# One 8 MB transfer per expert for the gate-up weights, in place of four of 2 MB

## The chip, the cores and the metric

The kernel runs on one core of one Trainium2 chip. The metric is the device time in microseconds (us) of one execution, as the median of several runs. The core has five engines that matter here: PE (TensorE, the matrix products), DVE (VectorE), ACT (ScalarE), POOL (GpSimd) and SP (SyncE), which computes nothing and issues the transfers from device memory (HBM) to on-chip memory (SBUF, 128 partitions). A transfer is spread over 16 DMA engines. They work through what SP has issued in the order of issue; each transfer adds to a semaphore when it has landed.

## The reference, cut to what matters

One decoder layer on 256 tokens of width 1024 in float32: a Mamba-2 mixer, a memory cross-attention, and a mixture of 32 experts of which each token takes four. Only the last part is touched, and it takes three quarters of the time, since all experts' weights have to be read once (8 MB of gate-up and 4 MB of down for each):

```
hn = rms_norm(h, ffn_norm)                       # 256 x 1024
top4 of hn @ w_router + b_router, gates = softmax(top logits)
for each expert e, for its tokens:
    gu   = hn @ w_gate_up[e] + b_gate_up[e]      # 1024 -> 2048
    act  = (clip(up) + 1) * gate * sigmoid(1.702 * gate)
    y   += gates[e] * (act @ w_down[e] + b_down[e])   # 1024 -> 1024
out = rms_norm(h + y, final_norm)
```

## The kernel before, in words

**Tiling.** An expert's tokens (up to 64 here) are gathered by a product of the normed tokens `xn` with a one-hot matrix, into `xs`: eight blocks of 128 features by 64 tokens. `gate_up` multiplies these eight blocks with eight blocks of 128 rows of the expert's 1024 x 2048 matrix; that is 64 products with 512 columns. `down` does the same with the activations and 32 products, `scatter` adds the gated result to the sums of all tokens.

**Which row lies on which partition.** The gate-up matrix of an expert is loaded as four pieces `s` = 0 to 3 of 256 rows, 2 MB each. Partition p gets the neighbouring rows 2p and 2p+1 of a piece, 16 KB that lie together in HBM. The normed tokens are written in an order that fits this (`norm_apply`, L1453: features dealt by two neighbours), and the gathers pick their blocks of `xn` by an index `k`.

**Buffers.** Even experts' pieces go to four slots of 16 KB per partition in `ring`; odd experts' pieces to four slots in three places: `mid` (two), the last third of `wring`, and `hs`. The down matrix has one set of two slots of 2 MB. So two experts' gate-up and one expert's down fit.

**Order on SP.** SP issues transfers in program order and waits before each until its slot has been read. `gu_used` counts pieces of gate-up that PE has used, `dn_used` pieces of down. From expert 3 on, a loop issues gate-up of expert e+2 (four transfers, each as soon as PE has used that piece of expert e; L362) and down of expert e (two transfers, each when that half of expert e-1's down has been used; L365). After the loop comes an order written out by hand: pieces 0 and 1 of gate-up 27, down 25, pieces 2 and 3 of gate-up 27, and then down 26, gate-up 28, down 27, gate-up 29, down 28, gate-up 30, down 29, gate-up 31. The down matrices of experts 30 and 31 come last, as eight transfers of 1 MB into the slots of gate-up 30 (L478).

**Order on PE.** For each expert c (`regular`): gate-up of c (L952; it waits for each piece at its first use), in odd experts half a gather (L928), down of c-1 (L980), the transposes of c's result (L967), scatter of c-1 (L990), in odd experts the other half of a gather. At the end `last_experts`: gate-up 31, then the four quarters of down 30 with the transposes between (L1003, L967, L1020), down 31 with the two scatters.

The functions that the change touches, with the numbers of the lines:

Of the kernel before, what the change touches and what calls it, by code (L numbers as in the profile page):

```python
# [55 lines left out]
GP, DP = 4, 2  # L56
RSLOTS = 8
# [5 lines left out]
def build(nc, x, mem, mixer_norm, xattn_norm, mem_norm, ffn_norm, w_in, conv_w, conv_b, dt_bias, a_log,  # L63
          d_skip, ssd_norm, w_out, xa_w_q, xa_w_kv, xa_w_o, w_router, b_router, w_gate_up, b_gate_up,
          w_down, b_down, final_norm, out):
    with ExitStack() as ctx:
# [16 lines left out]
        sq_at = hs_at + 4 * 2048  # L83

# [12 lines left out]

        act_lo = nc.alloc_sbuf_tensor_at("act_lo", [P, 12288], F32R, offset=ring_at)
# [258 lines left out]
        gu_dram = w_gate_up.rearrange("e (s p k) n -> e s p k n", p=P, k=2)  # L357
        dn_dram = w_down.rearrange("e (s p k) n -> e s p k n", p=P, k=4)

        def load_gate_up(sp, e, odd, s):  # L360
            n = GP * odd + s
            sp.dma_start(gu_w(n), gu_dram[e, s, :, :, :]).then_inc(g_ready[n], 16)  # L362
# [4 lines left out]
        def load_gate_up_row(sp, e, odd, s, kk):  # L367
            n = GP * odd + s
            sp.dma_start(gu_w(n)[:, kk:kk + 1, :], gu_dram[e, s, :, kk:kk + 1, :]).then_inc(g_ready[n], 16)
# [4 lines left out]

        def g_loads(n, c):


            return c // 2 + 1 + (1 if n > GP else 0 if n == GP or c < 2 else 1 if n else 2)
# [9 lines left out]
        def _(sp):  # L388
# [33 lines left out]
            load_gate_up(sp, 1, 1, 0)  # L422
# [5 lines left out]
            load_gate_up_row(sp, 1, 1, 1, 0)  # L428
            load_gate_up_row(sp, 1, 1, 2, 0)
            sp.wait_ge(wo_ps, 10)  # L430
            load_gate_up_row(sp, 1, 1, 1, 1)
# [6 lines left out]
            for a in range(2):  # L438
                sp.wait_ge(gu_part, a + 1)
                sp.dma_start(gu_w(0)[:, 0:1, 1024 * a:1024 * (a + 1)],  # L440
                             gu_dram[2, 0, :, 0:1, 1024 * a:1024 * (a + 1)]).then_inc(g_ready[0], 16)
# [20 lines left out]
            with sp.Fori(0, PAIRS - 4, 1) as i:  # L462
# [6 lines left out]
            for e in range(NE - 6, NE - 2):  # L469
                reload_down(e, 0, e)  # L470
                reload_gate_up(e + 2, 0, e + 2)
            sp.wait_ge(cnt_ps, 1)
# [62 lines left out]
        def _(pe):  # L535
# [383 lines left out]
            def gather_half(i, pair, half):  # L919
# [5 lines left out]
                for m in range(4):  # L925
                    k = 4 * (m // 2) + 2 * half + m % 2
# [12 lines left out]
            def gate_up(i, c, first=False):  # L939

                for s in range(GP):
# [3 lines left out]
                    pe.wait_ge(g_ready[n], 16 * i + 16 * g_loads(n, c))  # L945
# [62 lines left out]
            def last_experts(i):  # L1008
# [4 lines left out]
                gate_up(i, 1)  # L1013
# [944 lines left out]
```

## Time and profile before

| | |
|---|---|
| median of 3 runs | 1248.43 us (1248.24 to 1248.56) |
| the profiled execution | 1248.27 us |
| its span, first to last instruction | 1246.4 us |
| granted TensorE clock, mean | 0.996 |
| PE busy | 1172.7 us (94%) |
| DVE, ACT, POOL busy | 389.6, 276.1, 7.5 us |
| DMA queue of SP | 453.74 MB, 88.2% of 16 engines' span |

The profile shows one execution. The span is 1.9 us shorter than that execution's time, since what lies ahead of the first instruction and after the last isn't in it. PE's busy time says less than it seems to: products are pipelined and their ends are modelled, so a PE that waits a microsecond in thirty still shows 9 tenths. The share of the DMA engines is told by packets: one packet here is one contiguous run of bytes that goes to one partition (16 KB in the middle of the kernel), and each transfer adds one small packet per DMA engine, which moves the semaphore. Of an issued transfer the trace tells when SP issued it and how long after that it landed; in a full queue most of that is waiting behind earlier transfers.

### The profile page before, as it was taken

The numbers are of one execution on the slowest core, as the hardware profiler recorded it, in microseconds if no ns is written. First come the engines' busy times: TensorE is split into PE (matmuls) and PEld (weight loads), VectorE is DVE, ScalarE is ACT, GpSimd is POOL, SyncE is SP. The second block draws the span as 40 slices with busy tenths as digits, with TensorE's granted clock in tenths as the row PEclk, the third lists the DMA queues.
The fourth block names the chain that finished last, engine by engine and source line by source line (L and its number), as shares of the span: only waits on it lengthen the run. The fifth ranks groups of instructions, "written<-read, shape, count | busy, mean of one in ns | idle before, by whom it ended". The sixth has DMA issues, their size and how long they took to land.

```text
span 1246.4 us, 15481 instructions
## 1 busy us (share of the span) xinstructions
PE 1172.7 (94%) x6198; PEld 619.5 (50%) x6198; DVE 389.6 (31%) x703; ACT 276.1 (22%) x421; POOL 7.5 (1%) x27
## 2 busy tenths in 40 slices
PE   9999999999999999989989999899999998999996
PEld 8998887898633433333333333333433333333432
DVE  5987677546312111111111112102111111112112
ACT  5655566345211101010000101001101011011102
POOL 1000000000000000000000000000000000000000
PEclk9999999999999999999999999989999999999999
DMA  9454333469899999999999999999999999999996
GB/s 344 151 203 142 129 135 137 161 262 379 314 416 428 429 429 429 427 428 428 427 429 429 429 429 429 429 427 428 429 429 428 429 428 429 427 416 429 428 426 256
DMA packets 56966, 454.28 MB, mean 364 GB/s; under 512 B 6556, under 2 KB 6724, under 8 KB 30948
## 3 DMA queue, kind: packets, MB, share of 16 engines
q1 hardware_dynamic: 56752, 453.74, 88.2%
q8 instruction: 24, 0.39, 0.1%
q10 hardware_dynamic: 180, 0.07, 0.0%
q14 instruction: 10, 0.08, 0.0%
HBM read 452.74 MB, written 1.05 MB: 364 GB/s over the span
## 4 chain that ended last, share of the span: by engine, by line
PE 56%; DMA 41%; DVE 1%; issue 1%; SPq 1%; ACT 0%; DVEq 0%; POOL 0%; POOLq 0%
DMA ring<-in_moe_w_down 41%; PE ps L952 14%; PE ps L980 11%; PE ps L615 3%; PE ps L617 3%; PE ps L616 3%; PE ps L630 2%; PE ps L990 2%; PE ps L631 2%; PE ps L632 2%; PE ps L928 2%; PE ps L602 1%; PE ps L747 1%; PE ps L967 1%; PE ps L726 1%; PE ps L725 1%
## 5 line engine op out<-in xcount | busy, mean ns | idle before, releaser
L980 PE MATMUL ps<-ring,wring 128*64 128x512 f32 x960 | 216.5, 597 | 53.0 <-DMA ring<-in_moe_w_down 53.0
L952 PE MATMUL ps<-ring,wring 128*64 128x512 f32 x1024 | 223.5, 594 | 0.0
L1101 ACT ACTIVATE wring<-ps 128x512 f32<-128x512 f32 (+2 forms) x101 | 52.4, 534 | 496.2 <-PE ps L952 424.1
L980 PEld LDWEIGHTS ps<-ring,wring 128*64 128x64 f32 x960 | 65.1, 137 | 192.6 <-issue 112.2
L1828 DVE COPY wring<-ps 128x512 f32<-128x512 f32 x32 | 22.1, 692 | 402.7 <-PE ps L952 402.7
L952 PEld LDWEIGHTS ps<-ring,wring 128*64 128x64 f32 x1024 | 72.0, 137 | 139.3 <-issue 139.1
L1836 DVE TENSOR_TENSOR wring<-ps,bguT 128x512 f32<-128x512 f32 x64 | 41.2, 686 | 300.8 <-PE ps L967 300.8
L952 PE MATMUL ps<-mid,wring 128*64 128x512 f32 x512 | 115.2, 603 | 1.0 <-DVE wring L1836 1.0
L1101 ACT ACTIVATE ysb<-ps 128x512 f32<-128x512 f32 x36 | 21.4, 595 | 264.6 <-PE ps L980 250.3
L952 PEld LDWEIGHTS ps<-mid,wring 128*64 128x64 f32 x512 | 36.0, 139 | 69.0 <-issue 69.0
L928 PEld LDWEIGHTS ps<-wring 128*128 128x128 f32 x480 | 55.8, 192 | 23.5 <-issue 23.5
L990 PE MATMUL ps<-ysb,wring 64*128 64x512 f32 x256 | 63.6, 615 | 0.7 <-ACT ysb L1101 0.7
L928 PE MATMUL ps<-wring 128*128 128x128 f32 x480 | 61.6, 282 | 0.0
L952 PE MATMUL ps<-wring 128*64 128x512 f32 x256 | 57.7, 592 | 0.0
L952 PE MATMUL ps<-hs,wring 128*64 128x512 f32 x256 | 57.7, 592 | 0.0
L1469 DVE TENSOR_TENSOR wlo<-wring,lo_ring 128x2048 fp32r<-128x2048 f32 x23 | 52.2, 2287 | 11.3 <-ACT lo_ring L1101 11.3
L1101 ACT ACTIVATE lo_ring<-wring 128x2048 fp32r<-128x2048 f32 x24 | 45.5, 1932 | 9.9 <-PE ps L617 5.6
L632 PE MATMUL ps<-hi_ring,wlo 128*128 128x256 f32 x160 | 45.3, 283 | 0.0
L967 PEld LDWEIGHTS ps<-cst,wring 128*128 128x128 f32 x256 | 27.4, 141 | 26.9 <-issue 25.1
L616 PE MATMUL ps<-wlo,hi_ring 128*128 128x512 f32 x96 | 37.4, 390 | 0.0
L952 PEld LDWEIGHTS ps<-hs,wring 128*64 128x64 f32 x256 | 18.5, 137 | 36.4 <-issue 36.1
L952 PEld LDWEIGHTS ps<-wring 128*64 128x64 f32 x256 | 18.5, 137 | 36.4 <-issue 36.4
(316 smaller groups left out, 1416.0 us busy)
## 6 DMA issues: line engine op xcount, KB each, us to landing
ring<-in_moe_w_gate_up SPq DMA_DIRECT2D x60, 2048.0 KB, 23.1
ring<-in_moe_w_down SPq DMA_DIRECT2D x59, 2048.0 KB, 25.5
mid<-in_moe_w_gate_up SPq DMA_DIRECT2D x31, 2048.0 KB, 23.5
wring<-in_moe_w_gate_up SPq DMA_DIRECT2D x15, 2048.0 KB, 26.3
hs<-in_moe_w_gate_up SPq DMA_DIRECT2D x15, 2048.0 KB, 27.9
wring<-in_ssd_w_in SPq DMA_DIRECT2D x9, 2048.0 KB, 8.1
ring<-in_moe_w_down SPq DMA_DIRECT2D x10, 1024.0 KB, 33.1
wring<-in_xa_w_kv SPq DMA_DIRECT2D x4, 2048.0 KB, 8.0
```

The costliest lines, as they stand in the source:

```text
L615: mm(ps[bank][:, :], xh[:, k0 + k, tok], wh, start=start and k == 0, stop=False)
L616: mm(ps[bank][:, :], xh[:, k0 + k, tok], wl, start=False, stop=False)
L617: last = mm(ps[bank][:, :], xl[:, k0 + k, tok], wh, start=False, stop=stop and k == KD - 1)
L632: last = mm(dst, wl[:, c0:c0 + P], x_hl[0][:, k, :], start=False, stop=k == KD - 1)
L928: last = mm(ps[G_BANK][:, P * m:P * (m + 1)], xn[:, t, P * k:P * (k + 1)], onehot[:, t, :, :], start=t == 0, stop=t == TC - 1)
L952: last = mm(ps[a][SLOTS * half:SLOTS * (half + 1), :], xs[:, m, c % 2, :], w[:, kk, c0:c0 + 512], start=s + kk == 0, stop=s + kk == GP)
L967: last = tr(ps[a][:, P * j:P * (j + 1)], gus[:, c0:c0 + P], ident)
L980: last = mm(ps[D_BANK][SLOTS * half:SLOTS * (half + 1), :], act[:, k, :], w[:, kk, 512 * half:512 * (half + 1)], start=k == 0, stop=k == K ...
L990: last = mm(ps[4 + 2 * t + half][:, :], rows[r, P * t:P * (t + 1)], ysb[r, :], start=False, stop=True, skip_group_check=True)
L1101: return nc.scalar.activation(out_, in_, func, **kw)
L1469: v.tensor_tensor(lo_, raw_, hi.bitcast(F32), ALU.subtract).then_inc(wl_ok, 1)
L1836: v.tensor_tensor(gu[:, a, :, :, :], ps[a][:, :].rearrange("p (j h s) -> p j h s", j=4, h=2), b4[:, a, :, :].unsqueeze(3).to_broadcast([P, ...
```

## The change

From expert 4 to expert 30, gate-up comes as one transfer of 8 MB instead of four of 2 MB. For that,

- partition p gets the eight neighbouring rows 8p to 8p+7 of the expert's matrix, 64 KB that lie together in HBM (`GR` = 8). Features are dealt by eight neighbours in `norm_apply`, and the gathers' index `k` follows;
- the odd experts' four slots lie side by side as `odd_ring`, over the last third of `wring`, `mid` and `hs`. Slot 4 is now `wring`'s and slots 5 and 6 `mid`'s, and the first loads of expert 1 are issued for other slots accordingly;
- the group's transfer waits until all four pieces of the expert two before it have been used, and PE waits for the whole group ahead of an expert's first gate-up product;
- experts 0 to 3 and 31 are still loaded in pieces (or in single rows of 8 KB); a piece's 16 KB on a partition are now 64 KB away from those of the next partition. The first round of the loops on SP and PE is written out ahead of them;
- the order after the loop is down 25, gate-up 27, down 26, gate-up 28 and so on: no piece of gate-up 27 goes ahead of down 25 any more.

```diff
@@ buffers
+        odd_ring = nc.alloc_sbuf_tensor_at("odd_ring", [P, GP * WP], F32, offset=wring_at + 8 * WP)
         def gu_slot(n):
             if n < GP:
                 return slot(n)
-            return (part(mid, 0, WP), part(mid, WP, 2 * WP), wslot[2], hs[:, :])[n - GP]
+            return part(odd_ring, WP * (n - GP), WP * (n - GP + 1))
@@ loads
-        gu_dram = w_gate_up.rearrange("e (s p k) n -> e s p k n", p=P, k=2)
...
+        gu_rows = w_gate_up.rearrange("e (j p k) n -> e j p k n", p=P, k=GR)
+        def gu_dram(e, s, k0, k1):
+            return gu_rows[e, s // GS, :, 2 * (s % GS) + k0:2 * (s % GS) + k1, :]
...
+        def load_gate_up_group(sp, e, odd, j):
+            sp.dma_start(gu_group(odd, j), gu_rows[e, j, :, :, :]).then_inc(g_ready[GP * odd + GS * j], 16)
@@ SP
-            def reload_gate_up(e, i, c, pieces_=range(GP)):
-                for s in pieces_:
-                    sp.wait_ge(gu_used, 2 * GP * i + (GP * (c - 2) + s + 1))
-                    load_gate_up(sp, e, c % 2, s)
+            def reload_gate_up(e, i, c, groups=range(GJ)):
+                for j in groups:
+                    sp.wait_ge(gu_used, 2 * GP * i + (GP * (c - 2) + GS * (j + 1)))
+                    load_gate_up_group(sp, e, c % 2, j)
...
-            with sp.Fori(0, PAIRS - 4, 1) as i:
+            reload_pieces(3)
+            reload_down(1, 0, 1)
+            reload_gate_up(4, 0, 4)
+            reload_down(2, 0, 2)
+            with sp.Fori(1, PAIRS - 4, 1) as i:
...
-            reload_gate_up(NE - 5, 0, NE - 5, (0, 1))
+            reload_gate_up(NE - 5, 0, NE - 5, range(0, GJ // 2))
             reload_down(NE - 7, 0, NE - 7)
-            reload_gate_up(NE - 5, 0, NE - 5, (2, 3))
+            reload_gate_up(NE - 5, 0, NE - 5, range(GJ // 2, GJ))
@@ PE
-                    k = 4 * (m // 2) + 2 * half + m % 2
+                    k = 4 * half + 2 * (m % 2) + m // 2
...
-                    pe.wait_ge(g_ready[n], 16 * i + 16 * g_loads(n, c))
+                    pe.wait_ge(g_ready[n], 16 * i + 16 * g_loads(n, c) if n % GS == 0 else 16 * g_loads(n, expert))
@@ DVE, norm_apply
-                    v.scalar_tensor_tensor(out=dst[:, t, :].rearrange("q (k p) -> q k p", k=2),
-                                           in0=src[:, t, :].rearrange("q (p k) -> q k p", k=2), scalar=rst[:, n, t:t + 1],
+                    v.scalar_tensor_tensor(out=dst[:, t, :].rearrange("q (k p) -> q k p", k=GR),
+                                           in0=src[:, t, :].rearrange("q (p k) -> q k p", k=GR), scalar=rst[:, n, t:t + 1],
```

`GR` = 8, `GJ` = 1 and `GS` = 4, so a group is a whole expert, and `range(0, GJ // 2)` is empty.

The first place where this moves instructions is SP's queue around the reload of expert 4. Before, in the loop, two down transfers of expert 1 and then four gate-up transfers of expert 4, each with a wait of its own (two of the four are shown):

```order
L365 DMA ring<-in_moe_w_down 128x4096
L453 REGISTER_ALU
L362 ISA [waits gu_used]
L362 DMA ring<-in_moe_w_gate_up 128x4096
L453 REGISTER_ALU
L362 ISA [waits gu_used]
L362 DMA ring<-in_moe_w_gate_up 128x4096
```

Now, ahead of the loop, expert 3's four pieces, down 1, the whole of expert 4, and down 2:

```order
L468 DMA wring<-in_moe_b_down 32x1024
L376 DMA odd_ring<-in_moe_w_gate_up 128x4096 [waits gu_used] x4
L379 DMA ring<-in_moe_w_down 128x4096 [waits dn_used] x2
L390 DMA ring<-in_moe_w_gate_up 128x16384 [waits gu_used]
L379 DMA ring<-in_moe_w_down 128x4096 [waits dn_used] x2
```

The transfer of the last piece stands where it stood; those of the first three pieces moved back to it.

The second place is SP's queue behind the loop. Before (the first row is two pieces of gate-up 27, the second down 25):

```order
L362 DMA mid<-in_moe_w_gate_up 128x4096 [waits gu_used] x2
L365 DMA ring<-in_moe_w_down 128x4096 [waits dn_used] x2
L362 DMA wring<-in_moe_w_gate_up 128x4096 [waits gu_used]
L362 DMA hs<-in_moe_w_gate_up 128x4096 [waits gu_used]
L365 DMA ring<-in_moe_w_down 128x4096 [waits dn_used] x2
L362 DMA ring<-in_moe_w_gate_up 128x4096 [waits gu_used] x4
```

Now (the first row is down 25, the second gate-up 27, the last is expert 31 in pieces; the rows left out repeat the pair for experts 28 to 30):

```order
L379 DMA ring<-in_moe_w_down 128x4096 [waits dn_used] x2
L390 DMA odd_ring<-in_moe_w_gate_up 128x16384 [waits gu_used]
L379 DMA ring<-in_moe_w_down 128x4096 [waits dn_used] x2
L390 DMA ring<-in_moe_w_gate_up 128x16384 [waits gu_used]
...
L376 DMA odd_ring<-in_moe_w_gate_up 128x4096 [waits gu_used] x4
```

Gate-up 27 moved as a whole behind down 25.

## Rows read from the trace of the kernel before

**Rows 1.** The page's GB/s in 40 equal slices of 31.2 us.

```profile
GB/s 344 151 203 142 129 135 137 161 262 379 314 416 428 429 429 429 427 428 428 427 429 429 429 429 429 429 427 428 429 429 428 429 428 429 427 416 429 428 426 256
```

**Rows 2.** Waits of PE, whole span: us in total, times, longest us.

```profile
PE ps L980 <- DMA ring<-in_moe_w_down: 53.0, 37, 1.8
```

**Rows 3.** Chain that ended last, two neighbouring experts: start us, us, what.

```profile
653.78 3.68 PE ps L980 x16
...
683.14 3.68 PE ps L980 x16
```

**Rows 4.** DMA packets of stretches 440:1040, 1213:1230 and 248:252.

```profile
DMA packets 17656, 257.06 MB, mean 428 GB/s; under 512 B 1967, under 2 KB 1967, under 8 KB 1967
...
DMA packets 981, 7.15 MB, mean 421 GB/s; under 512 B 109, under 2 KB 109, under 8 KB 109
...
DMA packets 782, 1.60 MB, mean 400 GB/s; under 512 B 0, under 2 KB 0, under 8 KB 782
```

**Rows 5.** DMA issues of stretches 373:374, 277:278, 284:285: KB, us to landing.

```profile
ring<-in_moe_w_down SPq DMA_DIRECT2D x1, 2048.0 KB, 15.9
...
ring<-in_moe_w_down SPq DMA_DIRECT2D x1, 2048.0 KB, 7.5
...
ring<-in_moe_w_gate_up SPq DMA_DIRECT2D x1, 2048.0 KB, 7.6
```

**Rows 6.** Timeline of SP, reloads of down 1, gate-up 4: start us, us.

```profile
370.08 3.75 SPq L365 DMA_DIRECT2D ring<-in_moe_w_down  x2
382.24 10.62 SPq L362 DMA_DIRECT2D ring<-in_moe_w_gate_up  x4
```

**Rows 7.** Timeline of PE, first pieces of gate-up 1, and gate-up 2.

```profile
350.37 7.09 PE L952 MATMUL ps<-mid,wring 128*64 128x512 f32 x32 [1.02 <-DVE wring L1836]
...
378.40 13.95 PE L952 MATMUL ps<-ring,wring 128*64 128x512 f32 x64
```

**Rows 8.** Timeline of SP, gate-up reload of an even expert, steady part.

```profile
666.35 10.62 SPq L362 DMA_DIRECT2D ring<-in_moe_w_gate_up  x4
```

**Rows 9.** Timeline of SP, reload of down 25.

```profile
1063.68 5.22 SPq L365 DMA_DIRECT2D ring<-in_moe_w_down  x2
```

**Rows 10.** Chain that ended last, from down 24 to the end of down 31.

```profile
1064.88 3.65 PE ps L980 x16
...
1097.73 13.88 PE ps L952 x64
...
1125.76 13.88 PE ps L952 x64
...
1149.82 13.88 PE ps L952 x64
...
1177.84 13.91 PE ps L952 x64
...
1197.12 31.51 DMA ring<-in_moe_w_down
...
1232.53 3.61 PE ps L1003 x16
```

**Rows 11.** Line L478: its issues, and from issue to landing.

```profile
L478 SPq DMA_DIRECT2D ring<-in_moe_w_down x8: 328/3551/6242, 1181.5 to 1205.7; - x8
...
DMA to landing us min/median/max: 27.9/35.0/37.1
```

**Rows 12.** Timeline of PE, pieces of the end.

```profile
1216.25 1.94 PE L1003 MATMUL ps<-ring,wring 128*64 128x512 f32 x8 [0.46 <-DMA ring<-in_moe_w_down]
1218.12 1.09 PE L967 MATMUL ps<-cst,wring 128*128 128x128 f32 x8
1219.04 0.38 PE L1020 MATMUL ps<-cst,wring 128*128 128x128 f32 x2
...
1230.54 1.99 PE L990 MATMUL ps<-ysb,wring 64*128 64x512 f32 x8
```

**Rows 13.** Line L1453: count, duration ns min/median/max, first and last start us.

```profile
L1453 DVE SCALAR_TENSOR_TENSOR wring<-hs,rst x2: 1279/1282/1285, 322.9 to 326.9; 128x1024 f32<-128x1024 f32 x2
```

More of the change, by code:

```diff
@@ L56 @@
 GP, DP = 4, 2
+GR = 8
+GJ = 2 * GP // GR
+GS = GR // 2
 RSLOTS = 8
@@ L83, in build @@
         sq_at = hs_at + 4 * 2048
+        assert mid_at == wring_at + 12 * WP and hs_at == mid_at + 8 * WP
         def part(base, first, end, r=None, **sizes):
@@ L373, in load_down_rows @@
             sp.dma_start(dn_w(s)[:, rows, :], dn_dram[e, s, :, rows, :]).then_inc(d_ready[s], 16)
+        def load_gate_up_group(sp, e, odd, j):
+            sp.dma_start(gu_group(odd, j), gu_rows[e, j, :, :, :]).then_inc(g_ready[GP * odd + GS * j], 16)
         def g_loads(n, c):
-            return c // 2 + 1 + (1 if n > GP else 0 if n == GP or c < 2 else 1 if n else 2)
+            extra = (0 if n == GP + 1 else 1) if n >= GP else 0 if c < 2 else 1 if n else 2
+            if n % GS == 0:
+                return c // 2 + 1 + extra
+            return min(c // 2, 1) + 1 + extra + (1 if n >= GP and c >= NE - 1 else 0)
         def d_loads(s, c):
@@ L421, in _ @@
             sp.wait_ge(pv_ps, XH)
[L422 removed]
+            load_gate_up(sp, 1, 1, 1)
             sp.wait_ge(wo_half, 1)
@@ L465, in _ @@
                     reload_down(2 * i + c, i, c)
-            reload_gate_up(NE - 5, 0, NE - 5, (0, 1))
+            reload_gate_up(NE - 5, 0, NE - 5, range(0, GJ // 2))
             reload_down(NE - 7, 0, NE - 7)
-            reload_gate_up(NE - 5, 0, NE - 5, (2, 3))
-            for e in range(NE - 6, NE - 2):
+            reload_gate_up(NE - 5, 0, NE - 5, range(GJ // 2, GJ))
+            for e in range(NE - 6, NE - 3):
                 reload_down(e, 0, e)
                 reload_gate_up(e + 2, 0, e + 2)
+            reload_down(NE - 3, 0, NE - 3)
+            reload_pieces(NE - 1)
             sp.wait_ge(cnt_ps, 1)
@@ L925, in gather_half @@
                 for m in range(4):
-                    k = 4 * (m // 2) + 2 * half + m % 2
+                    k = 4 * half + 2 * (m % 2) + m // 2
                     for t in range(TC):
@@ L937, in scatter_transpose, with gate_up @@
                 last.then_inc(st_ps, 1)
-            def gate_up(i, c, first=False):
+            def gate_up(i, c, expert, first=False):
                 for s in range(GP):
@@ L1028, in last_experts, with regular @@
                 scatter(i, 1, scatT_last).then_inc(fin_ps, 1)
-            def regular(i, c, gathers=True):
+            def regular(i, c, expert, gathers=True):
                 scatter_transpose(i, c)
@@ L1034, in regular @@
                 pe.wait_ge(up_b, 2 * i + c)
-                gate_up(i, c)
+                gate_up(i, c, expert)
                 if gathers:
@@ L1071, in _ @@
             first_gather(1, (0, 1))
-            gate_up(0, 0, True)
+            gate_up(0, 0, 0, True)
             transposes(0, 0)
-            with pe.Fori(0, MIDDLE, 1) as i:
-                regular(i, 1)
-                regular(i, 2, False)
+            regular(0, 1, 1)
+            regular(0, 2, 2, False)
+            with pe.Fori(1, MIDDLE, 1) as i:
+                regular(i, 1, 3)
+                regular(i, 2, 4, False)
             biases_and_list()
```

27 lines of the change are left out of this document (17 added, 10 removed).

## The prediction

> **What bounds the kernel now.** First the slices of the page [rows 1]: from the thirteenth slice (about 375 us) to the last but one the DMA engines move 426 to 429 GB/s, slice after slice, with one dip to 416. A rate that stays the same over 27 experts is a limit, not a coincidence. Then the waits of PE [rows 2]: it waits 37 times for a down matrix, 53.0 us in total and never over 1.8 us. Then the chain that ended last [rows 3]: down of one expert begins at 653.78, of the next at 683.14. An expert has six transfers of 2 MB, so one takes 29.36 / 6 = 4.893 us. In this part PE isn't the bound, it is released by the last byte of each down matrix. So the kernel's end is set by one stream: whatever leaves the DMA engines idle after about 360 us is added to the time, and whatever makes a transfer shorter is taken off it.
>
> The chain changes towards the end [rows 10]: down 24 starts at 1064.88 on a landing, and then PE runs without a wait for a transfer until 1215.8 [rows 12], because the order behind the loop lets it run ahead of the down transfers. There PE and the stream finish nearly together, and either can be late.
>
> **What a longer packet saves.** Three stretches with a full queue have packets of different size [rows 4]. Time per data packet of one DMA engine is 16 x the stretch over the packets (all packets less the small ones): 16 x 600 / (17656 - 1967) = 611.9 ns at 16 KB, 16 x 17 / (981 - 109) = 311.9 ns at 8 KB, 16 x 4 / 782 = 81.8 ns at 2 KB. Twice the 8 KB packet less one of 16 KB leaves 11.9 ns that don't depend on bytes: the packet's own cost and an eighth of that of the semaphore's packet. Landings, which suffer less from the edges of a stretch, give a little less: the transfer issued at 1197.12 lands at 1228.63 [rows 10], the last, issued at 1205.7, 27.9 us later at 1233.6 [rows 11]; two transfers of 1 MB in 4.97 us against 4.893 for one of 2 MB, so a 2 MB transfer has about 0.08 us that isn't bytes (by the packets 8 x 11.9 ns = 0.095).
>
> Four transfers of 2 MB carry this four times; one of 8 MB with eight packets of 64 KB per DMA engine carries it once. Saving per expert: 3 x 0.08 = 0.24 us by landings, 3 x 0.095 = 0.29 us by packets. I take 0.24 and a group of 4 x 4.893 - 0.24 = 19.33 us. The end below zero: if 64 KB runs are in fact moved as packets of 16 KB, only three semaphore packets go. The 2 KB stretch, which holds no semaphore packet, has 81.8 - 300.0 / 4 = 6.8 ns of its own per packet, so the semaphore's costs 8 x (11.9 - 6.8) = 41 ns at most, and the saving is 0 to 0.12 us. A loss per group has no row that shows it; it is a rival below.
>
> The Trainium skill (DMA: Bandwidth & Descriptors, the section on the SWDGE anatomy of one DMA) fits a transfer's time as about 2.0 us plus its bytes over 436 GB/s, which read as a cost of each transfer would promise 6 us per expert. The trace differs for a full queue (4.893 us from one transfer to the next, 0.08 of it fixed) and shows such a cost only in an empty one, below.
>
> Experts 4 to 26 have landed when down 24 lands at 1064.84. That is 23 groups x 0.24 = 5.5 us off that moment.
>
> **The gap in front of expert 4.** Before, its four pieces are issued as PE uses those of expert 2: the issues begin at 382.24 and the last is at 382.24 + 10.62 - 0.33 = 392.53 [rows 6]. Down 1's second half, issued at 373.50 (370.08 + 3.75 - 0.33), lands 15.9 us later at 389.4 [rows 5, 6], and the pieces issued from 382.24 on are there by then and keep the stream going. Now the whole group waits for the last piece of expert 2, which PE reads at the end of 378.40 + 13.95 = 392.35 [rows 7]. Nothing else is in the queue: behind the waiting group stand down 2 and expert 5. A transfer into an empty queue takes 7.5 to 7.6 us to land [rows 5], 2.65 more than 4.893. So the stream starts again as if at 392.53 + 2.65 = 395.2, not at 389.4: a gap of 5.7 us. From there on the stream is what ends last, so all of it counts. +5.7.
>
> **The steady part has slack.** In an even expert the reload is issued last at 666.35 + 10.62 - 0.33 = 676.6 [rows 8], 22.9 us after down's second half started at 653.78 [rows 3]. Then 2.65 us until bytes move: 25.5. In the queue at 653.78 and behind it are a group and a down, 29.1 us. So a group that waits for all four pieces still comes 3.6 us before the queue is dry. If PE or the reload were 3.6 us later per expert, this cover would be gone. Nothing is charged. Expert 5 right after the gap has room too: the group lands at 395.2 + 19.3 = 414.5 and down 2 at 424.3, while gate-up 3 starts 24.1 us after gate-up 2 (as 29 after 28 where nothing waits [rows 10]), at 402.5, and has used its last piece at 416.4.
>
> **The end.** I follow the stream from down 24's landing, 1064.84, by 9.79 us for a down and 19.33 for a group. Down 25 now has no gate-up ahead of it and can't be issued before down 24's halves are used: first half at 1063.68 [rows 9], landing after 7.5 at 1071.2 (the stream alone would have given 1069.7, so a gap of 1.5), second half 1076.1. Then gate-up 27 lands at 1095.4, down 26 at 1105.2, gate-up 28 at 1124.5, down 27 at 1134.3, gate-up 29 at 1153.6, down 28 at 1163.4, gate-up 30 at 1182.8. PE is ready for the gate-ups 27 to 30 at 1097.73, 1125.76, 1149.82 and 1177.84 [rows 10]. It needed the last piece only some 10 us later; now it needs all at once. 27 and 28 are in time (28 by 1.2 us). 29 is late by 3.8 us; PE, thus delayed, is ready for 30 at 1181.7 and waits 1.1 more: 4.9 us in sum. Gate-up 31, in pieces, ends at 1215.8 + 4.9 = 1220.7. Behind it stand 64 products of down 30 and 31 at 13.88 / 64 = 0.217 us, so 13.9 us, and transposes and a scatter of about 1.0, 0.3 and 1.9 [rows 10, 12]: 1237.8. Before, the same work ended at 1232.53 + 3.61 = 1236.1, since half of PE's delay there was waiting for transfers, which is used up now; the last landing moves only from 1233.6 to 1234.2 and is no longer last. With some tenths for switching between these pieces I take the end +2.2 us against down 24's landing. With no saving at all per group it would be +3.1.
>
> **Small parts.** The exchange of slots 4 and 6 changes nothing in the order or size of the first loads; PE's first gate-up of expert 1 waits for DVE at 350.37, not for a transfer [rows 7]. The two operations that write the normed tokens read every second element and take 1.28 us each [rows 13]; reading every eighth I take the same, 0, and at most twice the time, +1.3 on the path of each, 2.6 in all; below zero there is nothing to gain. The rounds written out ahead of the loops add instructions to PE and SP, beside a stream that doesn't wait for them. The pieces of experts 0 to 3 and 31 keep their packets.
>
> **Sum.** +5.7 (gap) - 5.5 (23 groups) + 2.2 (end) = +2.4 us. The profiled execution took 1248.27 us, of which 1.9 lie outside the span and don't change; it stands 0.16 below the median of the runs, 1248.43. Forecast: 1250.9 us, slower by 0.2%, which is about what a measurement of this kernel can tell from no change (2.5 us).
>
> **The rivals.**
> - *The packets don't grow.* 64 KB runs are cut, or the cost goes with every 16 KB whatever the packet. For it: no packet over 16 KB is in the trace. Against: from 2 to 16 KB the cost follows the number of packets. Then +5.7 + 3.1 less 0 to 2.8 = +6.0 to +8.8; 1254.4 to 1257.2. Cut in two pieces of 32 KB it is about +4.
> - *Not slower: long packets save more than their count.* Place: the same groups. The slices say that rate still rises with size, 400, 421, 428 GB/s [rows 4]. At 0.29 us per group the sum is +1.1; from 0.34 on it is zero, and at 0.40 it is 5.7 + 2.0 - 9.2 = -1.5, 1246.9. To be faster by 2.5 us it takes 0.45. Against it: 0.34 would mean 8.39 MB in 19.23 us, 436 GB/s, which no full stretch here reaches.
> - *The 64 KB step between partitions slows the reads.* All DMA engines then read at addresses 64 KB and more apart, where it was 16 KB. No row here has such a step. Each per cent is 27 x 0.196 = 5.3 us; with the saving gone and one per cent lost it is +14, 1262. Against: at 16 KB apart the rate is flat over 27 experts [rows 1]. The Trainium skill (DMA: Bandwidth & Descriptors, Latency and other measured facts) lists copies that lose most of their rate when rows lie 4 MiB apart and 3% at 512 KiB; nothing in it is as short as 64 KB, and no run here shows it.
>
> **How the numbers follow.** Full saving, +2.4 with about 1 us either way: 0.50, half of it beyond 0.2% slower and half within. Packets that don't grow: 0.22, slower. More than the count: 0.22, of which 0.13 within 0.2% and 0.09 faster. The step: 0.06, slower. So faster 0.10, within 0.2% 0.37, slower 0.53. The likeliest case alone reaches from 1249.5 to 1252.5. The range goes down to 1246.5, where the third case is nearly used up, and up to 1257.5, the end of the second; outside lie most of the fourth case and a few hundredths of the third.
>
> **What would show it.** In the profile after: (1) no transfer issue between 374 and 392 us and a hole of 5 to 6 us in the stream near 390 to 395; (2) packets of 64 KB, their count down by 27 x 16 per expert with the small ones, a period of 29.36 - 0.24 = 29.12 us between two downs; (3) one short gap near 1065 and new waits of L952 for a transfer of about 4 and 1 us ahead of gate-up 29 and 30; (4) a last landing that PE no longer waits for. I am wrong if the period isn't 0.2 to 0.3 us shorter, if the hole isn't there or something downstream absorbs it, or if PE reaches gate-up 29 after its transfer.

## The result and the profile after

The changed kernel takes 1261.12 us (median of 4 runs, 1260.77 to 1263.47), against 1248.45 (1248.24 to 1248.56) for the kernel before on the same chip: ratio 1.0108, 95% interval 1.0096 to 1.012. It is 12.7 us slower. The forecast was +2.4 us and the range ended at 1257.5. The profiled execution took 1261.15 us with a span of 1259.4, so 12.9 us more than the one before.

First the page's slices, 31.5 us each (GB/s), to lay beside [rows 1]:

```profile
GB/s 345 146 200 157 121 124 134 195 267 357 329 418 351 432 416 430 432 428 432 437 433 433 433 433 433 431 359 438 431 413 427 433 432 433 395 419 432 432 422 217
```

The steady level has risen from 429 to about 432 (the mean of the eleven slices from the sixteenth on). That is the gain. But there are dips that weren't there: 351 in the thirteenth slice, 359 in the 27th (818 to 850 us), 395 in the 35th. The first is the predicted hole, the last is the predicted gap at the end. The forecast has nothing for the middle one, and a missing sixth of 31.5 us is more than 5 us.

The products with the second halves of the down matrices date it: PE starts them when the stream has landed them, so they tell how far the stream is. The rows are those of down 3, 4, 15, 17 and 24. The timeline of PE (start us, us, engine, line, out<-in, count, what ended the wait) of the kernel after:

```profile
454.75 3.65 PE L1013 MATMUL ps<-ring,wring 128*64 128x512 f32 x16 [1.24 <-DMA ring<-in_moe_w_down]
484.11 3.65 PE L1013 MATMUL ps<-ring,wring 128*64 128x512 f32 x16 [1.24 <-DMA ring<-in_moe_w_down]
...
804.68 3.65 PE L1013 MATMUL ps<-ring,wring 128*64 128x512 f32 x16 [1.24 <-DMA ring<-in_moe_w_down]
...
869.06 3.65 PE L1013 MATMUL ps<-ring,wring 128*64 128x512 f32 x16 [1.25 <-DMA ring<-in_moe_w_down]
...
1073.01 3.65 PE L1013 MATMUL ps<-ring,wring 128*64 128x512 f32 x16 [1.22 <-DMA ring<-in_moe_w_down]
```

and the halves of down 3, 4 and 15 before (that of down 24 starts at 1064.88, [rows 10]):

```profile
448.23 3.65 PE L980 MATMUL ps<-ring,wring 128*64 128x512 f32 x16 [0.36 <-DMA ring<-in_moe_w_down]
477.59 3.65 PE L980 MATMUL ps<-ring,wring 128*64 128x512 f32 x16 [1.24 <-DMA ring<-in_moe_w_down]
...
800.60 3.65 PE L980 MATMUL ps<-ring,wring 128*64 128x512 f32 x16 [1.24 <-DMA ring<-in_moe_w_down]
```

| at down of expert | after less before | what it holds |
|---|---|---|
| 4 | +6.5 us | the hole ahead of expert 4, less three groups' saving: 7.2 |
| 15 | +4.1 | eleven more groups: -2.4, 0.22 each |
| 17 | +9.7 (869.06 against 800.60 + 2 x 29.36) | 64.4 us for two experts in place of 58.3: +6.1 in one place |
| 24 | +8.1 | seven more groups: -1.6 |
| last product of down 31 | +13.0 (1245.52 against 1232.53) | the end: +4.9 |

For down 17 the stream's own pace is the comparison, since PE, held up in the middle, started it late before as well. So 7.2 + 6.1 - 5.1 (23 groups) + 4.9 = 13.1, of which 12.9 are seen in the profiled executions.

**The steady part.** The chain that ended last has a period of 513.25 - 484.11 = 29.14 us, where it was 29.36 [rows 3]:

```profile
484.11 3.68 PE ps L1013 x16
...
513.25 3.68 PE ps L1013 x16
```

A stretch inside it, 440:800, holds half as many packets as in the kernel before for the same bytes:

```profile
DMA packets 5428, 155.26 MB, mean 431 GB/s; under 512 B 608, under 2 KB 608, under 8 KB 608
```

```profile
DMA packets 10594, 154.21 MB, mean 428 GB/s; under 512 B 1182, under 2 KB 1182, under 8 KB 1182
```

The first is after, the second before. 64 KB on a partition travel as one packet.

**The hole ahead of expert 4.** Windows of the kernel after (stretch and its length, then busy us and count of PE, PEld, DVE, ACT, POOL, the granted clock, the DMA share, GB/s):

```profile
389.00:393.00 4.00, 4.00 (x20) 1.28 (x18) 0.15 (x1) 0.15 (x1) 0.00 (x0) 1.00 0.00 0
394.00:397.00 3.00, 3.00 (x18) 0.99 (x16) 0.00 (x0) 0.00 (x0) 0.00 (x0) 1.00 0.88 350
833.00:836.00 3.00, 3.00 (x17) 1.03 (x14) 0.25 (x1) 0.25 (x1) 0.00 (x0) 1.00 0.00 0
837.00:840.00 3.00, 3.00 (x19) 1.41 (x19) 0.00 (x0) 0.60 (x1) 0.00 (x0) 1.00 0.87 306
```

Before, the stretch 389:393 moved 422 GB/s. Now nothing moves in it, and when bytes flow again they do so at 350 GB/s for the first 3 us. SP's timeline shows why (start us, us, what):

```profile
373.81 0.33 SPq L379 DMA_DIRECT2D ring<-in_moe_w_down  x1
392.84 0.33 SPq L390 DMA_DIRECT2D ring<-in_moe_w_gate_up  x1
...
836.02 0.33 SPq L390 DMA_DIRECT2D odd_ring<-in_moe_w_gate_up  x1
```

No issue stands between 374 and 392 us, as forecast. The third row is the second hole.

**The hole behind the middle.** Timeline of PE of the kernel after:

```profile
811.20 0.39 PE L1081 MATMUL ps<-cst,gate 128*32 128x128 f32 x2
812.06 3.69 PE L1087 MATMUL ps<-wring 32*128 32x512 f32 x8 [0.46 <-ACT wring L1136]
819.67 0.68 PE L968 MATMUL ps<-cst,wring 128*128 128x128 f32 x2 [1.63 <-issue]
820.29 15.41 PE L985 MATMUL ps<-odd_ring,wring 128*64 128x512 f32 x64
```

Half-way through the experts PE breaks off for 8.5 us (811.2 to 819.7): it transposes the gates, adds the down biases of all experts to the sums, and works out with DVE the list of what the slots leave over (`biases_and_list`, L1048 to L1065 before). The kernel before has the same break, from 807.1 to 815.4, so this is no new work: gate-up 17 begins 15.4 us (816.01) after the second half of down 15 there and 15.6 us (820.29) here. Before, the pieces of gate-up 19 were issued one by one, as those of gate-up 17 had been read (the first two, and the last):

```profile
821.72 3.77 SPq L362 DMA_DIRECT2D mid<-in_moe_w_gate_up  x2
...
831.99 0.33 SPq L362 DMA_DIRECT2D hs<-in_moe_w_gate_up  x1
```

Now the group of expert 19 waits for the last of them, which PE reads at 820.29 + 15.41 = 835.7, and goes out at 836.02. By then the stream is dry: 830:833 still moves 229 GB/s, 833:836 nothing (the third window above).

**The end.** Timeline of PE of the kernel after, gate-ups 28 to 30, and the windows over the last two:

```profile
1134.66 13.95 PE L985 MATMUL ps<-ring,wring 128*64 128x512 f32 x64 [0.77 <-DMA ring<-in_moe_w_gate_up]
1163.81 16.02 PE L985 MATMUL ps<-odd_ring,wring 128*64 128x512 f32 x64 [5.02 <-DMA odd_ring<-in_moe_w_gate_up]
1193.90 13.95 PE L985 MATMUL ps<-ring,wring 128*64 128x512 f32 x64
```

```profile
1163.80:1180.00 16.20, 16.19 (x66) 5.13 (x67) 0.12 (x1) 0.12 (x1) 0.00 (x0) 0.87 1.04 447
1193.90:1208.00 14.10, 14.10 (x67) 4.77 (x68) 0.70 (x3) 0.86 (x3) 0.00 (x0) 1.00 1.01 429
```

PE waits 5.0 us ahead of gate-up 29, and the same 64 products then take 16.02 us where they take 13.95 elsewhere, with a granted clock of 0.87. A stretch partly at 1.2 GHz in place of 2.4 explains this, and costs 2.1 us on top of the wait. Behind this wait the chain that ended last holds no transfer any more: from 1163.81 us on, gate-up 29 to 31, the last down matrices and the scatters run back to back on PE.

### The profile page after: what moved, and what is told of

Read it like the earlier page. It is cut to its first block, busy times and chain, and to the rows that moved or that the text cites. A ratio compares the mean times of both kernels' runs of the same rounds, so it can differ in the third digit from the quotient of the medians.

```text
span 1259.4 us, 15124 instructions
## 1 busy us (share of the span) xinstructions
PE 1174.8 (93%) x6198; PEld 620.3 (49%) x6198; DVE 391.0 (31%) x703; ACT 276.3 (22%) x421; POOL 7.5 (1%) x27
## 4 chain that ended last, share of the span: by engine, by line
PE 51%; DMA 47%; issue 1%; DVE 1%; ACT 0%; DVEq 0%; SPq 0%; POOL 0%; POOLq 0%
DMA ring<-in_moe_w_down 44%; PE ps L1013 10%; PE ps L985 10%; PE ps L647 3%; PE ps L649 3%; PE ps L648 3%; DMA odd_ring<-in_moe_w_gate_up 3%; PE ps L662 2%; PE ps L663 2%; PE ps L664 2%; PE ps L1023 1%; PE ps L1036 1%; PE ps L634 1%; PE ps L960 1%; PE ps L779 1%
## 5 line engine op out<-in xcount | busy, mean ns | idle before, releaser
L985 PE MATMUL ps<-odd_ring,wring 128*64 128x512 f32 x1024 | 226.8, 601 | 5.8 <-DMA odd_ring<-in_moe_w_gate_up 5.0
L985 PEld LDWEIGHTS ps<-odd_ring,wring 128*64 128x64 f32 x1024 | 74.0, 139 | 147.5 <-issue 141.2
L1000 PE MATMUL ps<-cst,wring 128*128 128x128 f32 x256 | 34.9, 279 | 0.9 <-DVE wring L1863 0.9
L1136 ACT ACTIVATE wring<-wring 128x512 f32<-128x512 f32 x32 | 20.2, 630 | 60.7 <-DVE wring L1875 60.7
L1023 PEld LDWEIGHTS ps<-ysb,wring 64*128 64x128 f32 x256 | 22.0, 186 | 22.5 <-issue 20.9
L1538 DVE SCALAR_TENSOR_TENSOR ring<-ps,parT,ring 128x255 f32<-128x255 f32 (+2 forms) x72 | 31.1, 476 | 1.8
## 6 DMA issues: line engine op xcount, KB each, us to landing
ring<-in_moe_w_gate_up SPq DMA_DIRECT2D x4, 2048.0 KB, 12.9
```

The lines of the kernel that those rows point to most:

```text
L985: last = mm(ps[a][SLOTS * half:SLOTS * (half + 1), :], xs[:, m, c % 2, :], w[:, kk, c0:c0 + 512], start=s + kk == 0, stop=s + kk == GP)
L1000: last = tr(ps[a][:, P * j:P * (j + 1)], gus[:, c0:c0 + P], ident)
L1023: last = mm(ps[4 + 2 * t + half][:, :], rows[r, P * t:P * (t + 1)], ysb[r, :], start=False, stop=True, skip_group_check=True)
L1136: return nc.scalar.activation(out_, in_, func, **kw)
```

## The experiments

The theory, formed from this profile: a transfer that waits for all four pieces needs a stream that lags far behind PE, that is, a queue that still holds enough work when PE reads the last piece. PE uses the last piece about 10.4 us (three quarters of 13.9) after the first, and a start from an empty queue costs 2.65 us or more. Where the lag is there, the long transfer saves its 0.2 us. Where it isn't (at the start, behind PE's break, at the end), the stream runs dry for what is missing. The rivals: the long packets or the 64 KB step in HBM cost something themselves; the hole at 836 us has a cause other than PE's break; the small costs of the new order of the tokens matter.

**Experts 4, then 19, then 27 to 30 in pieces.** The changed kernel, with a table of experts whose gate-up comes in four pieces again (where neighbouring experts differ by it, the rounds of the loops on SP and PE are written out):

```diff
+PIECES = (4,)
```

> The changed kernel (1261.1 us) with expert 4's gate-up back in four pieces of 2 MB, everything else as changed. Theory A, idle gaps: the stream stands still for 6.2 us in front of expert 4 and lands the down transfer behind it 1.0 us late; both go, so 1254.1 us (7.0 less), and the gap near 835 us and that near 1073 us stay as they are. Rival B, the longer packets or the 64 KB step cost rate all along: a piece less among 27 groups changes the time by under 1 us, 1260 to 1261.

Measured 1257.45 us (1256.92 to 1258.6), ratio 1.0073 (1.0056 to 1.009), 3.7 less than the changed kernel. The stretch that had been empty is full, but a new hole opens one expert later, where the odd group is issued at 417.21 and lands 23.0 us later (windows of this kernel):

```profile
386.00:400.00 14.00, 14.00 (x69) 4.61 (x65) 0.69 (x1) 0.76 (x2) 0.00 (x0) 1.00 1.01 428
417.00:421.00 4.00, 4.00 (x26) 2.55 (x28) 0.69 (x1) 1.20 (x2) 0.00 (x0) 1.00 0.85 287
```

```diff
-PIECES = (4,)
+PIECES = (4, 19)
```

> Experts 4 and 19 in pieces. Theory A: the gap of 6.3 us near 835 us arises because PE is late there by the biases and the list of experts (about 8 us between down 16 and gate-up 17), and the whole group of expert 19 waits for the last piece of expert 17; with pieces the stream keeps running, so 6.0 us less than with expert 4 alone, about 1248.0. Rival B: no change against the run before beyond 1 us. Rival C, that the gap comes from something at that time on the DMA engines (code loading, say) and not from the wait: the gap stays near 835 us although pieces are issued from about 825 us on.

Measured 1258.12 us (1254.34 to 1259.67), ratio 1.0069 (1.0047 to 1.009): no gain over the one before. The hole moved and became a little shorter: two experts took 65.58 us around the break in the run before (800.11 to 865.69, 7.3 over 2 x 29.14), three take 93.30 here (802.14 to 895.44, 5.9 over). In the profiled execution that is used up by a later start of the experts' stage, 350.64 us in place of 348.42 (see what stays open). Its windows and SP's timeline:

```profile
832.00:842.00 10.00, 10.00 (x54) 4.34 (x52) 0.69 (x1) 1.19 (x2) 0.00 (x0) 1.00 1.00 428
858.00:868.00 10.00, 10.00 (x50) 3.29 (x47) 0.69 (x1) 0.60 (x1) 0.00 (x0) 1.00 0.62 242
```

```profile
862.62 0.33 SPq L393 DMA_DIRECT2D ring<-in_moe_w_gate_up  x1
```

The hole at 836 is gone and stands at 862, in front of expert 20. That one expert got through doesn't give the stream the lag that it lacks: the next group needs it just the same.

```diff
-PIECES = (4, 19)
+PIECES = (4, 19, 27, 28, 29, 30)     # and pieces 0 and 1 of gate-up 27 ahead of down 25 again
```

> Experts 4, 19 and 27 to 30 in pieces, and the order behind the loop as in the kernel before (two pieces of gate-up 27 ahead of down 25). Theory A: the end costs 4.9 us with groups (a gap of 3.3 us at down 25, 5.0 us of waiting at gate-up 29 and 2 us of slower clock behind that wait), all of it goes; 21 groups remain and save 0.24 us each, so about 1243.3 us, faster than the kernel before (1248.4) by 5. Rival B (the step of 64 KB costs rate): not under 1248.

Measured 1254.77 us (1251.51 to 1255.6), ratio 1.0043 (1.0029 to 1.0057). Its windows:

```profile
412.00:422.00 10.00, 10.00 (x54) 4.06 (x51) 0.69 (x1) 0.60 (x1) 0.00 (x0) 1.00 0.89 367
859.00:868.00 9.00, 9.00 (x44) 3.02 (x42) 0.69 (x1) 0.60 (x1) 0.00 (x0) 1.00 0.48 177
1070.00:1080.00 10.00, 8.76 (x50) 3.98 (x45) 3.25 (x6) 1.23 (x2) 0.00 (x0) 1.00 1.00 428
```

The end is mended, and the two moved holes stay, of about 1.4 and 5.7 us in this profile. They aren't all that keeps this kernel 5.8 us above the one before: in the profiled execution, which lies 7.3 above the one before, the experts' stage also begins 4.5 us later (352.10 against 347.60 us), and the 21 groups save 4.6.

**The hole's cause: moving PE's break.** The changed kernel with

```diff
-MIDDLE = 8
+MIDDLE = 5
```

> The changed kernel with PE's biases and list of experts moved from ahead of pair 8 to ahead of pair 5, nothing else. Theory A, PE is late there and the whole-group wait hands this on to the stream: the gap of 6.3 us at expert 19's reload (836 us) is gone and one of 5 to 7 us stands at expert 13's (near 661 us); the time stays 1261 within 1.5. Rival C, something else at that time: the gap stays near 835 us.

Measured 1261.72 and 1262.55 us, against 1248.25 for the kernel before (two other executions took 3094 and 4503 us, which no profile explains, so there are only these two and no ratio). Windows and the issue:

```profile
655.00:666.00 11.00, 11.00 (x60) 4.70 (x58) 0.69 (x1) 1.19 (x2) 0.00 (x0) 1.00 0.44 159
830.00:838.00 8.00, 6.57 (x40) 3.28 (x38) 0.69 (x1) 1.19 (x2) 0.00 (x0) 1.00 1.00 428
```

```profile
662.54 0.33 SPq L390 DMA_DIRECT2D odd_ring<-in_moe_w_gate_up  x1
```

The hole went with the break, from 836 to 662 us, and the time stayed. So the cause is PE's break, and nothing tied to expert 19 or to that moment.

**How much is a hole's first expert, and how much the next ones.** Pieces for three experts at the start:

```diff
-PIECES = (4,)
+PIECES = (4, 5, 6)
```

> The changed kernel with experts 4, 5 and 6 in pieces (expert 4 alone gave 1257.4, and left a gap of 2.2 us in front of expert 5 and one of 0.5 behind it). Theory A'', the missing lag has grown to what a whole group needs by expert 7, since PE gains about 3 us per expert on the stream: no gap over 0.3 us up to 800 us, 2.7 us less than with expert 4 alone, plus 0.5 for two groups fewer: 1255.2 us. If gaps only move on, a gap of 2 us stands in front of expert 7 and the time is 1257.5 to 1258.

Measured 1256.69 us (1255.0 to 1258.8), ratio 1.007 (1.0057 to 1.0084). In 414:424 the stream runs at 428 GB/s. By its profile no hole follows at expert 7, so the lag had come by then, while the middle and the end cost what they did. The median is only 0.8 below that of the first experiment, but it comes from five executions between 1255.0 and 1258.8. In the profiles down 24 comes 1.8 us earlier (1067.87 against 1069.66), about what the hole of 2 us less two groups' saving gives.

**The layout alone, and the waits alone.** First the changed layout (token order, side-by-side slots, 64 KB step) with every expert in pieces and the order of before:

```diff
-PIECES = (4,)
+PIECES = tuple(range(4, 31))
```

> The changed layout (features dealt by eight, 64 KB step between partitions, odd slots side by side) with all experts in pieces of 2 MB and the order of the kernel before: only the layout differs from the kernel before. Theory A: 1248.4 us within 0.6, the layout costs nothing. Rival B, the step between partitions lowers the rate: over 1249.5; one per cent would be 1253.6. A rate of 428 GB/s in the steady part says A.

Measured 1249.92 us (1248.64 to 1252.41, 10 runs), ratio 1.0013 (1.0003 to 1.0022). In 440:800 the rate is what it was before, and eleven experts take 323.01 us in both kernels (second halves of down 4 and down 15, 477.87 to 800.88 here, 477.59 to 800.60 before):

```profile
DMA packets 10595, 154.23 MB, mean 428 GB/s; under 512 B 1182, under 2 KB 1182, under 8 KB 1182
```

Then the reverse: the kernel before with only the coarse waits and the order of the change, still four transfers of 2 MB:

```diff
-    sp.wait_ge(gu_used, 2 * GP * i + (GP * (c - 2) + s + 1))
+    sp.wait_ge(gu_used, 2 * GP * i + (GP * (c - 2) + (GP if whole else s + 1)))
```

and PE waits for all four `g_ready` ahead of an expert's first product. (It does so from expert 1 on, not only from 4; gate-up 2 starts at 378.42 us as it did at 378.40, so this cost nothing.)

> The kernel before with only the waits of the changed one: from expert 4 to 30 all four 2 MB transfers wait for the last piece of the expert two before, PE waits for all four before an expert's first product, and down 25 goes ahead of gate-up 27; packets, layout and number of transfers as before. Theory A: the same gaps near 390, 835 and 1065 us and the same waits at the end as the changed kernel, and none of its savings (5.5 us up to down 24): 1265 to 1267 us. Rival B, the loss comes from long packets or the 64 KB step: near 1249.

Measured 1267.87 us (1265.72 to 1268.04), ratio 1.0158 (1.0141 to 1.0175), 19.6 us over the kernel before. Windows and PE's wait:

```profile
389.00:394.00 5.00, 5.00 (x26) 1.66 (x24) 0.69 (x1) 0.60 (x1) 0.00 (x0) 1.00 0.26 52
832.00:842.00 10.00, 10.00 (x56) 4.41 (x54) 0.69 (x1) 1.19 (x2) 0.00 (x0) 1.00 0.45 152
```

```profile
PE ps L959 <- DMA hs<-in_moe_w_gate_up: 5.2, 1, 5.2
```

The same holes and the same wait of 5 us. So the waits and the order alone cost 19.6, and the changed kernel, with one transfer and packets of 64 KB in place of four, gives back 6.9 of it (19.6 less 12.7, each against its own chip's kernel before; the profiled executions say 4.6, and 27 groups at 0.22 would be 5.9). Only the size of this is loose: the two intervals, 1.0096 to 1.012 and 1.0141 to 1.0175, don't touch. The rival that long packets and the 64 KB step together cost more than they save is refuted.

**Where the 1.0 us of the layout comes from.** The changed kernel with two neighbours and pieces' worth of groups:

```diff
-GR = 8
+GR = 2
-k = 4 * half + 2 * (m % 2) + m // 2
+k = 4 * (m // 2) + 2 * half + m % 2
```

> The changed kernel with rows dealt by two neighbours again (16 KB that lie together, 16 KB step between partitions, transfers of 2 MB), but with the odd slots side by side, the exchanged first loads and the rounds written out ahead of the loops. Where the layout alone cost 1.0 us: if the 64 KB step is what costs, this runs as the kernel before, 1248.3 within 0.5, and without the spread of 3 us between runs. If slots, first loads or code cost it, 1249.3.

Measured 1248.42 us (1247.25 to 1249.69) against 1248.14: ratio 1.0000 (0.9991 to 1.0009). The slots side by side and the written-out rounds cost nothing that this can tell (the interval is 1.1 us either way). The operation that writes the normed tokens tells the rest (duration ns min/median/max, first and last start), first in this kernel, then after, to compare with [rows 13]:

```profile
L1488 DVE SCALAR_TENSOR_TENSOR wring<-hs,rst x2: 1279/1282/1284, 322.8 to 326.9; 128x1024 f32<-128x1024 f32 x2
```

```profile
L1488 DVE SCALAR_TENSOR_TENSOR wring<-hs,rst x2: 2075/2091/2107, 322.7 to 326.8; 128x1024 f32<-128x1024 f32 x2
```

Reading every eighth element takes 2.09 us, every second 1.28. The last transfer ahead of the reloads goes out at 348.29 us after, at 347.60 before and at 347.51 in this kernel, so 0.7 us of the 1.0 is seen here; the rest isn't explained, and with intervals of about 1 us it may be nothing. That the step in HBM costs rate is refuted by the 323.01 us above.

**A finer wait: 4 MB groups.** With `GR` = 4 a group is half an expert. The same edit also makes `range(0, GJ // 2)` hold one group, so the first half of gate-up 27 goes ahead of down 25 again, as in the kernel before; the waits are finer everywhere, and the end has the older order. If the missing lag is the cause, a group of two pieces needs only one piece's time (3.5 us) of lag and should have no holes:

```diff
-GR = 8
+GR = 4
-k = 4 * half + 2 * (m % 2) + m // 2
+k = 4 * (m % 2) + 2 * (m // 2) + half
```

> Groups of half an expert: rows dealt by four neighbours, 4 MB per transfer, 32 KB per partition that lie together; order and waits as the changed kernel has them with two groups per expert. Theory A': a reload may be issued about 7 us earlier and PE waits for half as much at once, so no idle stream at experts 4, 5, 19 and 20 and no wait at 29. Two transfers less per expert save 2 x 0.08 = 0.16 us, 27 times, 4.3 us: 1244.6 us against 1248.9 for the kernel before on this chip, or 1245.5 if the layout costs what the layout alone cost (1.0). Rival B, packets over 16 KB cost rate or starting time: 1248 or more.

Measured 1246.12 us (1244.61 to 1247.38, 10 runs) against 1248.25: ratio 0.9984 (0.9975 to 0.9994). Windows over both places and PE's waits for the down matrices:

```profile
389.00:394.00 5.00, 5.00 (x26) 1.71 (x24) 0.69 (x1) 0.60 (x1) 0.00 (x0) 1.00 1.02 439
832.00:842.00 10.00, 10.00 (x51) 3.83 (x49) 1.86 (x4) 1.31 (x3) 0.00 (x0) 1.00 1.02 439
```

```profile
PE ps L1013 <- DMA ring<-in_moe_w_down: 49.9, 37, 1.7
```

```profile
1062.05 3.65 PE L1013 MATMUL ps<-ring,wring 128*64 128x512 f32 x16 [1.24 <-DMA ring<-in_moe_w_down]
```

Both places are full, nothing waits for a gate-up, and down 24's second half starts 2.8 us earlier than before. This profile is of the fastest of its ten executions. It was run again unchanged on another chip:

> The kernel of half-expert groups once more, as the comparison for the run before on the same chip: 0.998 of the kernel before, 1245.5 to 1246.5 us; the two operations at 2.09 us each.

Measured 1245.95 us (1244.65 to 1247.85, 11 runs) against 1248.35: ratio 0.9983 (0.9974 to 0.9992). This version beats the kernel before by 0.2% and the changed one by 1.2%. The profile of this second run is of a slower execution (1247.14 us) and shows where it loses:

```profile
450.35 5.35 PE L1013 MATMUL ps<-ring,wring 128*64 128x512 f32 x16 [1.99 <-DMA ring<-in_moe_w_down]
```

The first time, the same products (those of down 3's second half) started at 448.49 and took 3.65 us. Here the half landed later and PE's granted clock was 0.72 in 450:456. From there to down 24 the two executions stay 1.85 us apart.

**Halves only where they are needed.** Expert 4 in four pieces; 5, 6, 19 to 22 and 27 to 30 in halves; the rest whole; the order of before around down 25:

```diff
+PIECES = (4,)
+HALVES = (5, 6, 19, 20, 21, 22, 27, 28, 29, 30)
```

> The changed layout, expert 4 in pieces of 2 MB, experts 5, 6, 19 to 22 and 27 to 30 in two transfers of 4 MB (32 KB per partition, 64 KB step), the other 16 of the 27 whole, and the order of the kernel before around down 25. Theory A'', the group wait needs a stream that lags PE by some 13 us, and where it doesn't (start, behind the biases, end) the missing lag is paid as idle stream at whichever expert comes first: with the small transfers in all those places no gap over 0.5 us is left, and 16 x 0.24 + 10 x 0.16 = 5.4 us are saved less 1.0 for the layout: 1244.5 us. Rival B, long packets cost more than they save: 1248 or more.

Measured 1247.85 us (1246.27 to 1251.01, 10 runs), ratio 0.9997 (0.9988 to 1.0007). It has no hole in the middle (429 GB/s in 832:842) and still isn't faster than 4 MB throughout, though more of its groups are whole. Its profile is of the slowest of its ten executions (1251.01 us), and in it the stage before the experts ends later:

```profile
353.06 0.43 SPq L498 DMA_DIRECT2D wring<-in_moe_b_down  x1
```

against 347.60 before. PE had waited 2.2 us for DVE once in that stage (0.6 in the first experiment). From this moment to the end this execution is 2.6 us shorter than that of the kernel before. Nothing that this experiment edits lies in that stage; its program is longer than the others, and whether that is the cause wasn't tested.

**The cost of the stepped read, moved to the write.** The 4 MB version with the loops of that one DVE operation turned (those of its other input too, which isn't shown), so that it reads neighbours and writes every 256th element:

```diff
-    out=dst[:, t, :].rearrange("q (k p) -> q k p", k=GR), in0=src[:, t, :].rearrange("q (p k) -> q k p", k=GR)
+    out=dst[:, t, :].rearrange("q (k p) -> q p k", k=GR), in0=src[:, t, :].rearrange("q (p k) -> q p k", k=GR)
```

> Half-expert groups (rows dealt by four) with the loop order of the two operations that write the normed tokens turned round: they read neighbouring elements and write with a step, where until now they read with a step of 4 or 8 and took 2.09 us each in place of 1.28 at a step of 2. Theory D, the reading step is what made them slower and that is the 0.7 to 0.8 us by which the experts' stage starts later in all kernels of the changed layout: 1.3 us each and 0.7 us off the time. Rival, a step costs on the writing side as well: 2.1 us each or more, and the time as the same kernel without the edit or later.

Measured 1246.86 us (1244.87 to 1247.69, 11 runs), ratio 0.9988 (0.9979 to 0.9997): no gain over the 4 MB version. Line L1488 in it:

```profile
L1488 DVE SCALAR_TENSOR_TENSOR wring<-hs,rst x2: 1995/2028/2062, 322.7 to 326.8; 128x1024 f32<-128x1024 f32 x2
```

The step costs nearly the same on the writing side, so turning the loops doesn't help.

## Why the prediction was wrong

**The failed step is "The steady part has slack ... Nothing is charged".** For an ordinary expert it holds: the group comes in time, and PE isn't even seen to wait for it. But it was checked on ordinary experts alone. The same paragraph named the condition ("if PE or the reload were 3.6 us later per expert, this cover would be gone") and didn't look for the one place where PE is later, though its instructions stood in the profile of before. By the paragraph's own sum the rows of the kernel before give it: the last piece of expert 19 is issued at 831.99, 31.4 us after down 15's second half started (800.60), and 2.65 us more make 34.0 against 29.1 in the queue, so 4.9 us short where 3.6 to spare were assumed. The break makes a hole of 6.1 us; the group that starts it lands 23.4 us after its issue and not 22.0, which is about the difference. Moving it moves the hole (`MIDDLE` = 5), and groups that need less lag have no hole there. Charged at 4.9 the sum would have been +7.3, at the measured 6.1 +8.5, instead of +2.4. The rest of the miss (10.5 us in the profiled executions) is 1.5 at expert 4, 2.7 at the end and 0.4 of saving, 10.7 in sum.

**The hole ahead of expert 4** was forecast in its place and with its cause, and mis-sized: 5.7 against 7.2. Its own terms give 5.8 (395.2 less 389.4). Issue at 392.84 instead of 392.53 is 0.3 of it. The group landed 22.0 us after its issue, as 19.33 + 2.65 = 22.0 had it. About 1 us is in down 2 behind it: PE waits 2.27 us for its second half, where 1.24 us is usual. And what the forecast didn't see is that this gap belongs to no expert: taking it from expert 4 gave it to expert 5.

**The end** was forecast as +2.2 and is +4.9. The waits, forecast as 3.8 and 1.1 us ahead of gate-ups 29 and 30, are 0.8 and 5.0 ahead of 28 and 29, with none at 30. What was missing is the clock: 2.1 us of slower products behind the 5 us wait. The gap at down 25 is longer, too: its halves go out at 1071.83 and, by its last issue, 1076.7, landing 7.8 and 9.4 us later. The second lands at 1086.1, 13.1 us behind down 24 (1072.97) where the stream alone takes 9.8: 3.3 us, where one gap of 1.5 us was forecast.

```profile
1071.83 5.21 SPq L379 DMA_DIRECT2D ring<-in_moe_w_down  x2
```

**The saving per group** was right: 29.12 forecast, 29.14 measured, by packets of 64 KB, and that the last landing no longer counts was right as well. Over 23 groups it is 5.1 us where 5.5 stood in the sum. "The packets don't grow" and "more than the count" are both refuted.

**The 64 KB step.** The rate at a step of 64 KB with 16 KB runs is 428 GB/s, as with neighbouring runs, and eleven experts take the same 323.01 us. The layout's kernel lies 0.13% (1.0 us) over the one before; 0.7 us of this is the later start behind the DVE operations. The Trainium skill (DMA: Bandwidth & Descriptors, Latency and other measured facts) lists losses for steps of 512 KiB and more in HBM; at 64 KB these runs show none.

**Small parts.** The operations that write the tokens were taken at 0 with up to 1.3 us each kept as a bound. They cost 0.8 us each and moved the experts' stage by 0.7 us in this kernel. At gate-up 2 PE is still 0.4 us late (378.84 against 378.40), and the 0.3 us by which group 4 is issued late, counted above, come from this.

**What stays open.** In the first experiment the time gained less than the holes alone would say, because the hole behind the break grew from 6.1 to 7.3 us: PE's granted clock over the 26 us from there is 0.80 in place of 0.87, and with slower products there 32.7 us in place of 31.3 pass until the group is issued. Why it is lower in that program isn't known. Programs with the most rounds written out also start the experts' stage later in their profiled executions: the transfer that goes out at 348.3 to 348.4 us in the changed kernel and with one or three experts in pieces goes out at 350.64, 352.10 and 353.06 with 4 and 19, with 4, 19 and 27 to 30, and with halves. Already the first wide stretch shows it (SP's issues near 109 us are 2.1 and 3.2 us late in the last two), long before any edited instruction. There is one profile of each, and this was not separated further. The medians may hold such starts as well, so differences of a microsecond or two between them say little.

## What to carry to other kernels

A wait made coarser is paid from the lag between consumer and stream, and that lag must be looked up at its smallest: at the first rounds, behind each thing that interrupts the consumer, and at the end, not in a typical round. An interruption that the stream bridged before the change, as it did PE's break here, has to be counted again. A hole isn't cured by exempting the round that shows it, since the next one needs the same lag. Of the sizes tried here the best was the largest whose wait the smallest lag covers: 4 MB, which saved 0.14 us per expert (period 29.22 in place of 29.36) and has no hole in its profile, where 8 MB saved 0.22 and paid 18 us.

## What the runs showed of the hardware

- A run of 64 KB on one partition is one packet. With 8 and 16 KB packets the stream moved 421 and 428 GB/s [rows 4]. For 64 KB packets 433 GB/s is an estimate: 8.39 MB in 29.14 - 9.79 = 19.35 us.
- A group of 8 MB that meets an empty queue lands after 22.0 to 23.4 us, where it takes about 19.3 of the stream in a full one, and the first 3 us run at 306 to 350 GB/s.
- PE's granted clock was 0.87 in the 16 us behind one wait of 5.0 us, seen after as 16.02 for 13.95 us of products, and in the first experiment too:

```profile
1160.10 16.50 PE L1050 MATMUL ps<-odd_ring,wring 128*64 128x512 f32 x64 [5.01 <-DMA odd_ring<-in_moe_w_gate_up]
```

  It fell behind PE's break too, and in the kernel before already: 0.81 in 808:816, where short products alternate with waits for DVE, and gate-up 17 took 15.7 us there. A wait of 1.99 us came with 0.72 in the 6 us around and behind it (4 MB groups, second run), while behind a wait of 2.27 us in the changed kernel (425.75) the products took their usual 3.65 us.

- DVE takes 1.28 us for 1024 float32 a partition when it reads every second element, 2.09 when every fourth or eighth, and 2.03 when it writes with a step.
